# Sparse attention: eight samples laid one by one between the first eight prompt groups, with the normalising on GpSimd

## The reference, cut to what matters

```python
def index_scores(qi, wi, ki):
    s = jax.nn.relu(jnp.einsum('bthd,bsd->bths', qi, ki).astype(jnp.float32))
    return jnp.einsum('bth,bths->bts', wi.astype(jnp.float32), s)
...
        sc = jnp.where(kpos[None, None, :] <= tpos[None, :, None], sc, -jnp.inf)
        _, idx = lax.top_k(sc, topk)                       # topk = 256
        valid = idx <= tpos[None, :, None]
        return sparse_attend(q_b, k[bidx, idx], v[bidx, idx], valid)
...
def sparse_attend(q, kg, vg, valid):
    s = jnp.einsum('btkgd,btjkd->btkgj', qg, kg).astype(jnp.float32) * HEAD_DIM ** -0.5
    s = jnp.where(valid[:, :, None, None, :], s, -1e30)
    pr = jax.nn.softmax(s, axis=-1)
    o = jnp.einsum('btkgj,btjkd->btkgd', pr.astype(vg.dtype), vg)
```

## Time and profile before

| | us |
|---|---|
| median of 3 runs (lowest to highest) | 3252.92 (3252.11 to 3254.89) |
| the profiled execution | 3254.98 |
| its span, first to last instruction | 3253.2 |
| attention, from the search to the samples' last output | 1745 to 2335 of the span |

### The profile page before, as it was taken

One profiled execution on the slowest core, in us unless ns is written; L12 is line 12 of the kernel. 1 busy time (PEld: TensorE's weight loads), 2 busy tenths in 40 slices (PEclk: granted clock), 3 DMA queues, 4 the chain that ended last, 5 costly groups with the idle time before them and its releaser, 6 DMA issues.

```text
span 3253.2 us, 43038 instructions
## 1 busy us (share of the span) xinstructions
PE 2950.3 (91%) x17384; PEld 2735.1 (84%) x17393; DVE 1403.7 (43%) x1868; ACT 749.3 (23%) x1158; POOL 936.0 (29%) x561
## 2 busy tenths in 40 slices
PE   5989899978899999999989946898798999999996
PEld 5889779968899999999977933446698999999995
DVE  6568266653422222212568887531134222222225
ACT  3353323320200011100235552332202100001111
POOL 2334223303343333334321310000032344333331
PEclk8999989969999999999999967997699999999998
DMA  4112100012111111111311120003210111111111
GB/s 146 39 33 60 29 26 1 1 57 71 30 48 47 45 39 42 45 45 48 107 38 37 46 82 1 26 10 105 83 45 26 46 49 45 48 40 42 42 44 66
DMA packets 237233, 153.09 MB, mean 47 GB/s; under 512 B 21243, under 2 KB 232884, under 8 KB 236169
## 3 DMA queue, kind: packets, MB, share of 16 engines
q1 hardware_dynamic: 226000, 121.17, 13.1%
q10 hardware_dynamic: 11116, 30.33, 2.6%
HBM read 133.46 MB, written 18.01 MB: 47 GB/s over the span
## 4 chain that ended last, share of the span: by engine, by line
PE 78%; DVE 13%; ACT 6%; issue 1%; DMA 0%; ACTq 0%; DVEq 0%
PE ps L1435 59%; ACT junk L898 3%; PE ps L720 2%; PE ps L789 2%; PE ps L753 2%; PE ps L1602 1%; PE ps L1587 1%; PE ps L1606 1%; DVE hl L2512 1%; DVE uc L2165 1%; PE ps L822 1%; PE ps L1512 1%; DVE mx L1169 1%; PE ps L747 1%; DVE cnt L1124 1%
## 5 line engine op out<-in xcount | busy, mean ns | idle before, releaser
L1331 POOL TENSOR_TENSOR w_hi<-w_raw,ones 128x512 fp32r<-128x512 f32 (+1 forms) x250 | 373.5, 1494 | 2023.9 <-PE ps L1435 1908.9
L1435 PE MATMUL ps<-xh,w_hi 128*128 128x352 f32 x2928 | 645.6, 329 | 68.1 <-DVE xl L2463 23.4
L1435 PE MATMUL ps<-xl,w_hi 128*128 128x352 f32 x2928 | 636.3, 326 | 0.0
L1435 PE MATMUL ps<-xh,w_lo 128*128 128x352 f32 x2928 | 635.4, 325 | 0.0
L1435 PEld LDWEIGHTS ps<-xh,w_hi 128*128 128x128 f32 x2928 | 505.0, 191 | 76.8 <-issue 63.2
L1435 PEld LDWEIGHTS ps<-xh,w_lo 128*128 128x128 f32 x2928 | 507.3, 189 | 0.0
L1435 PEld LDWEIGHTS ps<-xl,w_hi 128*128 128x128 f32 x2928 | 503.0, 190 | 0.0
L1334 POOL TENSOR_TENSOR w_lo<-w_raw,w_hi 128x512 fp32r<-128x512 f32 (+1 forms) x250 | 491.9, 1968 | 19.6
L2528 DVE TENSOR_TENSOR x<-x,ps 128x1056 f32<-128x1056 f32 x128 | 160.6, 1254 | 502.0 <-PE ps L1435 502.0
L2063 ACT ACTIVATE hs<-hu 128x1056 f32<-128x1056 f32 x64 | 69.7, 1090 | 1253.4 <-DVE hu L2504 1253.4
L1435 PE MATMUL ps<-hh,w_hi 128*128 128x352 f32 x1536 | 333.2, 325 | 13.7 <-DVE hl L2512 13.7
(11 more groups left out here) (374 smaller groups left out, 3035.6 us busy)
## 6 DMA issues: line engine op xcount, KB each, us to landing
w_raw<-in_w_up SPq DMA_DIRECT2D x64, 512.0 KB, 4.1
w_raw<-in_w_down SPq DMA_DIRECT2D x128, 256.0 KB, 2.7
w_raw<-in_w_in_rec SPq DMA_DIRECT2D x24, 512.0 KB, 3.9
x_spill<-x ACTq DMA_DIRECT2D x2, 4224.0 KB, 12.8
x<-x_spill ACTq DMA_DIRECT2D x4, 2112.0 KB, 7.6
w_raw<-in_w_in_att SPq DMA_DIRECT2D x16, 512.0 KB, 3.8
kpg<-in_cache_k SPq DMA_DIRECT2D x64, 128.0 KB, 2.0
vpg<-in_cache_v SPq DMA_DIRECT2D x64, 128.0 KB, 2.0
```

Source lines behind the costliest of these rows:

```text
L1331: pool.tensor_tensor(w_hi[:, j % 2, 0:n], w_raw[:, j % 2, 0:n], ones[:, 0:1].to_broadcast([P, n]), ALU.mult).then_inc(w_hi_done, 1)
L1435: mm = pe.matmul(ps[:, 3 * (j % 2) + t, 0:n], w[:, j % 2, k * P:(k + 1) * P], r[:, k, c0:c0 + n], start=(k == 0 and p == 0), stop=(k == kt ...
```

## The change

**The samples.** They are taken one at a time in eight steps t = 0 to 7. A step holds the scores of prompt group t, the values of group t - 1, the scores of sample t, the turns and values of sample t - 1, and the turning of sample t + 1's page keys. TensorE, VectorE and ScalarE each have the order of a step written out by hand. A sample's scores go through one PSUM bank in three pieces of 352 columns; each piece has its own maximum and its own exponential, and three factors per row (`s_fac`) bring the pieces to a common scale. Groups 8 to 15 follow with scores(n + 1) before values(n), as before; the last sample's turns and values stand among the scores of group 8.

**The normalising.** VectorE takes four reciprocals in one instruction (`reciprocals`) and works out the factors of a sample (`factors`); GpSimd does all products (`normalise`, four instructions a group, and `normalise_sample`, three a sample), and splits the output projection's weights only behind group 15.

**The search.** The small links are three (`cnt`, `carry`, `trial`); `cand` is updated beside them through a table `flips` made ahead of the search. A unit is taken out behind `trial`, after bits 0, 2, 5, 7 and so on to 26. Of the two counts behind the search one is left, over the three wider sets, and the token turns and copies move behind the search: on ScalarE four tokens' copies, two exponentials of group 0, the other copies, the six stores, then the first sample's page keys.

**The masks.** They hold 0 and minus 2^100 and are made in two halves, `mask_low` and `mask_high`; the samples' mask comes first, those of prompt blocks 2 to 5 in steps 0, 2, 4 and 6, and those of blocks 6 and 7 at groups 8 and 10.

**The loads.** SyncE issues the pages of samples 0 and 1 ahead of the groups, then in turn the keys of one sample (when a key buffer has been turned) and the values of another (when its value buffer has been used; there are two of these, which lie where the input projection's weights lay, and three key buffers). The loads of the output projection's weights wait for the last sample's values; the first two of them stood ahead of the search.

```diff
-        evict_after = {2 * u + 1: N_IDX + u for u in range(U_ATT_IN - N_IDX)}
-        FIRST_COPY = 25
+        evict_after = {(47 * u + 6) // 20: N_IDX + u for u in range(U_ATT_IN - N_IDX)}
+        N_TOK = QB + 3
...
             for u in range(N_IDX + 2, U_ATT_IN):
                 columns_in(u)
-            first = FIRST["att_out"]
-            units(sp, first, 2, 2, load(lambda j, off: w_out_att[:, :, ds((j + off - first) * P, P)], KT))
-            sp.wait_ge(S["tk_mm"], QB + 1)
             sp.wait_ge(S["trial_r"], 1)
-            for b in range(4):
+            for b in range(2):
                 page_loads(kpg[b], k_pages, b, S[f"kp_in{b}"])
-            sp.wait_ge(S["mask_r"], NB)
+            sp.wait_ge(mm_out, first + U_ATT_IN + 2)
             for b in range(2):
                 page_loads(vpg[b], v_pages, b, S[f"vp_in{b}"])
-            sp.wait_ge(S["at_pv"], steps_before[GROUPS])
-            for b in range(2, 4):
-                page_loads(vpg[b], v_pages, b, S[f"vp_in{b}"])
-            for pair in (4, 6):
-                for b in (pair, pair + 1):
-                    sp.wait_ge(S["sa_tr"], 4 * (b - 4) + 4)
-                    page_loads(kpg[b - 4], k_pages, b, S[f"kp_in{b - 4}"])
-                for b in (pair, pair + 1):
-                    sp.wait_ge(S["vp_used"], b - 3)
-                    page_loads(vpg[b - 4], v_pages, b, S[f"vp_in{b - 4}"])
-            units(sp, first + 2, U_ATT_OUT - 2, 2,
-                  load(lambda j, off: w_out_att[:, :, ds((j + off - first) * P, P)], KT))
+            sp.wait_ge(S["tk_mm"], N_TOK)
+            page_loads(kpg[2], k_pages, 2, S["kp_in2"])
+            for b in range(3, DEC_BATCH):
+                sp.wait_ge(S["sa_tr"], 4 * (b - 3) + 4)
+                page_loads(kpg[b % 3], k_pages, b, S[f"kp_in{b % 3}"])
+                sp.wait_ge(S["vp_used"], b - 2)
+                page_loads(vpg[(b - 1) % 2], v_pages, b - 1, S[f"vp_in{(b - 1) % 2}"])
+            sp.wait_ge(S["vp_used"], DEC_BATCH - 1)
+            page_loads(vpg[(DEC_BATCH - 1) % 2], v_pages, DEC_BATCH - 1, S[f"vp_in{(DEC_BATCH - 1) % 2}"])
+            first = FIRST["att_out"]
+            sp.wait_ge(S["vp_used"], DEC_BATCH)
+            units(sp, first, U_ATT_OUT, 2, load(lambda j, off: w_out_att[:, :, ds((j + off - first) * P, P)], KT))
             mlp_loads(sp, 1, load)
...
+            def normalise(n):
+                w = P * (n // KV + 1)
+                pool.wait_ge(S["rd_r"], recip_at(n))
+                for g in range(GRP):
+                    a = n * GRP + g
+                    pool.tensor_scalar(pr[n % 2][:, g, 0:w], pr[n % 2][:, g, 0:w], rden[:, a % 8:a % 8 + 1], None, ALU.mult)\
+                        .then_inc(S["at_nrm"], 1)
+
+            def normalise_sample(b):
+                pool.wait_ge(S["rd_r"], factors_at(b))
+                for p, (c0, cn) in enumerate(CUTS352):
+                    piece = pr_s[b % 2][:, c0:c0 + cn]
+                    ins = pool.tensor_scalar(piece, piece, s_fac[:, b % 2, p:p + 1], None, ALU.mult)
+                    if p < 2:
+                        pool_own.did(ins)
+                    else:
+                        ins.then_inc(S["at_nrm"], 1)
+
+            for n in range(GROUPS):
+                normalise(n)
+                if n < DEC_BATCH:
+                    normalise_sample(n)
+            pool.wait_ge(S["vp_used"], DEC_BATCH)
...
+            def sample_scores(b, p):
+                if p == 0:
+                    pe.wait_ge(S["sa_kts"], 4 * b + 4)
...
+                past = min(cn, PAST - c0)
+                pe.matmul(ps[0:64, 1, 0:cn], esel_b[:, b // 2, 64 * (b % 2):64 * (b % 2) + 64], mb_s[:, c0:c0 + cn],
+                          start=True, stop=False, skip_group_check=True)
+                for kv in range(KV):
+                    rows_q = slice(32 * kv, 32 * kv + 16)
+                    q_rows = qs[:, b, GRP * kv:GRP * (kv + 1), :].rearrange("p h t -> p (h t)")
+                    mm = pe.matmul(ps[rows_q, 1, 0:past], q_rows, kts[(b + 1) % 2][:, kv, c0:c0 + past], start=False, stop=True,
+                                   skip_group_check=True)
+                    if past < cn:
+                        mm = pe.matmul(ps[rows_q, 1, past:cn], q_rows, oq[:, 8 + kv, SEQ:TOK], start=False, stop=True,
+                                       skip_group_check=True)
+                mm.then_inc(S["sa_mm"], 1)
+
...
+                n = t - 1
+                last = n // KV + 1
+                if t:
+                    scores_head(t, 0)
+                if t + 1 < DEC_BATCH:
+                    page_keys(t + 1, 0)
+                if t:
+                    scores_head(t, 1)
+                sample_scores(t, 0)
+                scores_head(t, 2)
+                if t + 1 < DEC_BATCH:
+                    page_keys(t + 1, 1)
+                scores_head(t, 3)
+                if t:
+                    sample_turns(t - 1)
+                    values_step(n, 0)
+                sample_scores(t, 1)
+                if t + 1 < DEC_BATCH:
+                    page_keys(t + 1, 2)
+                if t:
+                    values_step(n, 1)
+                    sample_values(t - 1, 0)
+                sample_scores(t, 2)
+                if t and last >= 2:
+                    values_step(n, 2)
+                if t + 1 < DEC_BATCH:
+                    page_keys(t + 1, 3)
+                if t:
+                    sample_values(t - 1, 1)
+                    for k in range(3, last + 1):
+                        values_step(n, k)
+
...
+
             def bit(k):
-                dve.tensor_tensor(trial[:, :], cand[:, :], bits[:, k:k + 1].to_broadcast([P, NB]), ALU.bitwise_or)\
-                    .then_inc(S["trial_r"], 1)
                 dve.wait_ge(S["trial_r"], k + 1)
+                own.did(dve.tensor_tensor(cand[:, :], trial[:, :], flips[:, k, :], ALU.bitwise_xor))
                 count(trial, ALU.is_ge, DVE_Q)
                 dve.wait_ge(S["signs_r"], k + 1)
                 own.then(dve.scalar_tensor_tensor(cnt[:, act_cols], signs[:, :], -0.5, half_w[:, :], ALU.mult, ALU.add))
-                own.then(dve.scalar_tensor_tensor(acc[:, :], cnt[:, :], float(TOPK), neg[:, :], ALU.is_ge, ALU.not_equal))
-                own.then(dve.tensor_scalar(carry[:, :], acc[:, :], 2.0 ** (BITS - 1 - k), None, ALU.mult))
-                own.then(dve.tensor_tensor(cand[:, :], cand[:, :], carry[:, :], ALU.bitwise_or))
+                own.then(dve.tensor_scalar(carry[:, :], cnt[:, :], float(TOPK), 2.0 ** (BITS - 1 - k), ALU.is_ge, ALU.mult))
+                if k < BITS - 1:
+                    dve.tensor_tensor(trial[:, :], cand[:, :], carry[:, :], ALU.bitwise_xor).then_inc(S["trial_r"], 1)
+                else:
+                    own.then(dve.tensor_tensor(cand[:, :], cand[:, :], carry[:, :], ALU.bitwise_xor))
 
             for k in range(BITS):
                 bit(k)
...
+            def mask_low(k):
+                q, s, m, pn, w, eq, pre, low = mask_parts(k)
+                lim = cand[0:pn, q:q + 1].bitcast(F32)
+                own.did(dve.tensor_scalar(low, s, lim, 0.0, ALU.is_le, ALU.add, accum_out=cnt[0:pn, q:q + 1]))
+                own.then(dve.tensor_scalar(eq, s, lim, HUGE, ALU.is_equal, ALU.mult))
+                own.did(dve.tensor_scalar(quota[0:pn, q:q + 1], cnt[0:pn, q:q + 1], float(TOPK - w), HUGE, ALU.add, ALU.mult))
+                own.then(dve.tensor_tensor_scan(pre, ones[0:pn, 0:1].to_broadcast([pn, w]), eq, 0.0, ALU.mult, ALU.add))
+
+            def mask_high(k):
+                q, s, m, pn, w, eq, pre, low = mask_parts(k)
+                own.then(dve.scalar_tensor_tensor(eq, pre, quota[0:pn, q:q + 1], eq, ALU.is_le, ALU.mult))
+                dve.scalar_tensor_tensor(m, low, -HUGE, eq, ALU.mult, ALU.add).then_inc(S["mask_r"], 1)
+                dve.wait_ge(S["mask_r"], k + 1)
+
...
+            mask(0)
+            for t in range(DEC_BATCH):
+                for g in range(2):
+                    if t:
+                        head_max(t * GRP + g)
+                sample_max(t, 0)
+                for g in range(2, 4):
+                    head_max(t * GRP + g)
+                if t:
+                    first_copy(t - 1)
+                sample_max(t, 1)
+                reciprocals(t)
+                if t % 2 == 0:
+                    mask_low(t // 2 + 1)
+                sample_max(t, 2)
+                overall_max(t)
+                if t:
+                    output(t - 1)
+                    sample_output(t - 1)
+                factors(t)
+                if t % 2 == 0:
+                    mask_high(t // 2 + 1)
+
```

559 lines of the change are left out of this document (306 added, 253 removed).

## The result

The changed kernel takes **3161.68 us** (median of 4 runs, 3159.58 to 3162.08) where the kernel before, measured beside it, takes 3253.90: a ratio of 0.9716 with a 95% interval of 0.9699 to 0.9733, faster by 92 us. The forecast was 3158 us, with a range of 3128 to 3196. The profiled execution took 3162.08 us with a span of 3160.1; in the trace the gain over the kernel before is 3253.2 - 3160.1 = 93.1 us, where the sum said 94.8. One of run 10's six executions, at 4139.52 us and a granted clock of 0.643, was in a second, slower state; its ratio and the median given for it leave that one out.

The account below looks back on a forecast made before the run. The prediction saw TensorE waiting for VectorE in the first groups and often at a lower clock in the samples' stretch. Terms -146.3 - 17.5 + 68.0 + 1 = -94.8 from 3254.98, less 2.06, gave 3158 us, range 3128 to 3196.

Parts of the forecast that it names:

- What bounds the steps: Steps 1 to 7: TensorE's own work, 112.8 us at 2.4 GHz, with waits on top, 142.6 us in all.
- hand-overs: Steps 1 to 7: waits between engines that nothing covers, three or four a step, 2.0 us, so 14 us.
- The start and step 0: From the last bit: start 21 us, chained by ScalarE's copies and stores, then 10.5 us for the first step.
- The last step: Values of group 7, scores of group 8, last sample's turns and values, and 4.4 us of waits: 20 us.
- The search: Three links a bit instead of five and counts beside evictions: -17.5 us, bounds -10 and -20.
- Groups 9 to 15: Late prompt groups, already TensorE's; GpSimd's 7.6 us of products a group covered by 12 to 19 us: +1 us.
- signs of a wrong forecast: The forecast is wrong if the start takes more than 30 us or if the values wait for GpSimd.
- (a): Rival: hand-overs between engines, not TensorE, or slower loads bind the steps, 23 to 28 us each: 3178 to 3213; chance 0.25.
- (b): Rival: streams cover each other, TensorE nearly gapless, steps of 16.1 us: 3115 to 3140; chance 0.10.
- (c): Rival: GpSimd and VectorE hold each other up in every mask, 21 us, 2 already counted: 3177; chance 0.10.
- (d): Rival: narrow products in every step keep TensorE at 1.2 GHz, slower than before: 3286; chance 0.03.
- (e): Rival: samples don't go under the groups' time; steps of 34 us give back the gain, near 3253; chance 0.02.

Follow-up runs that it names:

- run 10: Run 9 with the twelve units between the search's bits taken out every 2.55 bits instead of 2.35: 3135.53 us, ratio 0.9625.
- run 8: Changed kernel with a sample's second-key-group value products cut to one of eight pages and the new keys, output partly wrong: 3150.64 us, ratio 0.9678.
- run 2: Changed kernel, but GpSimd splits only 64 of 1024 weight columns for the ten units beside the bits, so values are wrong: 3151.47 us, ratio 0.9681.
- run 4: Changed kernel with all four search links reading at most one operand from SBUF, carry written to PSUM: 3154.38 us, ratio 0.9686.
- run 5: Changed kernel with VectorE instead of GpSimd normalising prompt groups 8 to 15: 3161.68 us, ratio 0.9717.
- run 7: Changed kernel with all products on VectorE and the output projection's weights split by GpSimd only behind group 15: 3168.55 us, ratio 0.9729.
- run 6: Changed kernel with VectorE normalising groups 8 to 15 and GpSimd splitting the output projection's weights only behind group 15: 3158.38 us, ratio 0.9708.
- run 3: Changed kernel with only the links cnt and trial reading one operand from PSUM, token turns on three banks: 3168.04 us, ratio 0.9733.
- run 9: Changed kernel with the edits of run 4 and run 6 together: 3153.84 us, ratio 0.9682.

## Why the prediction was right

**What bounds the steps** was right, and is shown by run 8: TensorE's work, with short waits on top. TensorE was busy for 93% of steps 1 to 7 where I expected four fifths, at a mean clock of 0.90 instead of 0.95. Mis-sized are the waits: for hand-overs (14 us), the stretches of `factors` and `mask_high` (6.3), the page loads (3.5) and the holds (2) I had 25.8 us in sum, and TensorE's idle time there is 9.4. That the rest lay beside the other stream's work is the likely reason; no run separates the four. TensorE's busy time went the other way, 122.8 us for the 112.8 and 6 for the clock that I had: in steps 2 to 4 the clock is 0.81 to 0.83. Together that is the 12 us.

**The start and step 0** (28.7 against 31.5) went as worked out, with ScalarE's copies and stores as the chain: the 7.15 us in which ScalarE issues are the longest wait in the stretch. **The last step** took 22.3 instead of 20.

**The search** is the mis-sized term: -7.3, outside its bounds of -10 to -20. The working by links was right, 4.12 us for a quiet bit. The step that failed is the one on GpSimd: I had seen a hold of 1.4 us in the earlier trace rows, put 2 us of holds into the steps behind, and left them out of the search, as though they stayed what they were. They grew from 17.8 to 23.4 us as the order of the links moved, and the first two evictions waited 4.3 us for TensorE; that is 5.6 and 4.3 of the missing 10.2 us. Making the table `flips` ahead of the search, 0.9 us, wasn't in the sum either. Runs 2 and 4 show that without holds the search ends where it was forecast.

Two rows I had read wrongly. In the earlier trace rows the last two of the twelve units are the output projection's: the changed kernel splits ten in the search, the last at 1864.26, and those two behind the samples. The forecast time of the last unit held in run 4 all the same. And I wrote that no run shows a one-input instruction being held. The trace of the kernel before has one, until `w_lo` beside it ended (1760.24 + 2.40 = 1762.64):

```profile
1760.42 2.26 DVE L1126 TENSOR_SCALAR carry<-acc 128x7 int32<-128x7 f32 x1
```

**Groups 9 to 15** is the next one: +7.2 against +1. A product with a scalar on GpSimd wasn't in the trace, and I took the cost of two inputs, 1.04 us for 512 columns, for the upper bound. It is dearer than that, also where no mask of VectorE's lies beside it: 1.56 us in the second group of 512 columns. GpSimd's groups by shape in the changed kernel, from 1900 to 2260 (busy us, mean ns, then idle before):

```profile
L631 POOL TENSOR_SCALAR pr_s<-pr_s,s_fac 64x352 f32<-64x352 f32 x24 | 29.6, 1242 | 32.5 <-DVE s_fac L1384 32.5
L624 POOL TENSOR_SCALAR pr<-pr,rden 128x1024 f32<-128x1024 f32 x8 | 22.6, 2843 | 19.2 <-DVE rden L1359 19.2
...
L624 POOL TENSOR_SCALAR pr<-pr,rden 128x512 f32<-128x512 f32 x8 | 13.8, 1743 | 9.7 <-DVE rden L1359 9.7
...
L624 POOL TENSOR_SCALAR pr<-pr,rden 128x128 f32<-128x128 f32 x8 | 5.2, 665 | 78.3 <-DVE rden L1359 78.3
```

A step holds up to 11.1 us of GpSimd instead of 6.3. In the steps the cover was wide enough for that. Behind them I had 7.6 us for a group of 1024 columns, which took 11.3, with 12 to 19 us of TensorE's work in front, and that didn't cover the products of two of the eight groups. TensorE's timeline, groups 8 and 15:

```profile
2109.97 1.09 PE L801 MATMUL ps<-ident,pr 128*128 128x128 f32 x8 [2.51 <-POOL pr L624]
...
2230.15 1.09 PE L801 MATMUL ps<-ident,pr 128*128 128x128 f32 x8 [2.31 <-POOL pr L624]
```

That is 4.8 us; group 15 has nothing behind it that could be done first. So one of my signs of a wrong forecast, that the values wait for GpSimd, came true on a small scale. The other 2.4 us are not in the waits: TensorE's busy time in these groups is 125.14 us instead of 122.49, at a clock of 0.99 instead of 1.00.

**The rivals.** (a), the chain of hand-overs, is excluded by TensorE's 93% and by run 8. (b), nearly gapless, has the busy share nearly right but not the time: TensorE's busy time is 122.8 us and not 112.8. (c): its mechanism is there, but the 23 us of it lie in the search, where the rival didn't look; in the steps it is small: the four products of 512 columns took 7.6 us in a group with a mask beside them and 6.2 in the other. In run 5 it took 3.4 us in one group. (d): the clock fell to 0.81 to 0.83 in three of the seven steps, and in none to 0.5. Value products stand between wide ones there; the lowest clock in the windows above, 0.63, is behind the last bit, where TensorE is busy for 16.89 of 28.69 us. (e) is excluded by the result.

That the total came within 2 us owes something to errors of opposite sign: the search and the late groups cost 16 us more than forecast, and the steps and the start 15 less.

## What to carry to other kernels

In these runs a link of seven columns on VectorE that read SBUF alone lasted until the GpSimd instruction beside it ended, up to 2.3 us instead of 0.17. Take one operand of every link from PSUM (or put the result of a one-input link there), not of some, since the hold moves to the next link that can be held. When a chain gets shorter, lay the work that is threaded through it at the pace of its supplier again: with the same instructions, twelve evictions moved by one to three bits were worth 14 us by the traces and 18.6 by the ratios. And a pass that is moved to an idle engine is free only where other work covers it: in the steps TensorE waited for none of GpSimd's products of the groups, and behind them it waited 4.8 us. What GpSimd's part is worth as a whole, the 4.2 us of run 7, the intervals don't tell from nothing. Price the operation by its own row, not by a cousin's.

## What the runs showed that was not expected

- GpSimd's product with a scalar from SBUF to SBUF takes 0.60 us for 128 columns, 1.56 for 512 and 2.84 for 1024 where no mask lies beside it (the means of the rows above take in groups with a mask): longer than its products of two inputs in the earlier trace rows, 1.04 for 512 and 1.90 for 1024.
- One-input VectorE instructions from SBUF to SBUF are held by GpSimd too: 1.88 us for 128x7, and four products of 128x640 took 5.36 us instead of 1.94.
- TensorE's granted clock in the first step, which follows a start full of waits, differs between kernels whose step is alike: 0.94 in runs 4 and 6, 0.84 in the changed kernel, 0.76 in run 10, 0.67 in runs 3 and 9; between runs 4 and 9, which have the same instructions up to there, that is 6.7 us. One profile of each is all there is on that, and it is as large as some of the effects that the runs were made for.
